# Zeros in more of TensorE's pauses, and filter spectra over even and odd tokens apart

## The reference, cut to what matters

```python
def hyena_filter_spectra(z, window, w1, b1, w2, b2, w3, b3, freq):
    h = sin(freq[0] * (z @ w1 + b1)); h = sin(freq[1] * (h @ w2 + b2))
    h = (h @ w3 + b3).reshape(L, HY_ORDER, 2, HY_WIDTH) * window[:, None, None, :]
    fwd, bwd = h[:, :, 0], h[:, :, 1]
    f = concatenate([fwd, zeros, bwd[1:][::-1]], axis=0)
    f = f / (sum(abs(f), axis=0, keepdims=True) + EPS)
    return rfft(f, axis=0)
```

## Time and profile before

| | |
|---|---|
| runs | 2994.73, 2994.0, 2991.17 us; median 2994.0 |
| profiled execution | 2988.92 us, span 2987.1 us |
| mean granted clock | 0.967 |
| busy share of the span | PE 94%, DVE 67%, ACT 51%, POOL 2% |

### The profile page before, as it was taken

One profiled execution on the slowest core, in us unless ns is written; L12 is line 12 of the kernel. 1 busy time (PEld: TensorE's weight loads), 2 busy tenths in 40 slices (PEclk: granted clock), 3 DMA queues, 4 the chain that ended last, 5 costly groups with the idle time before them and its releaser, 6 DMA issues. The chain is left out here.

```text
span 2987.1 us, 43738 instructions
## 1 busy us (share of the span) xinstructions
PE 2808.3 (94%) x17891; PEld 2482.1 (83%) x17891; DVE 2004.8 (67%) x2003; ACT 1514.4 (51%) x1456; POOL 68.8 (2%) x55
## 2 busy tenths in 40 slices
PE   5899998699999999999998989999899899989999
PEld 5799998588888888888886578999899788989898
DVE  6555565588888888888785466665555666666555
ACT  3444353466667676667663325444434326443442
POOL 1000000000000000000000210000000110000000
PEclk8899989699999999999999899999999999999999
DMA  6155540399999999999997234444355433444353
GB/s 188 61 180 192 177 155 16 121 365 331 368 329 349 347 334 364 328 366 334 340 356 233 94 97 127 142 155 142 113 178 190 147 111 102 150 147 141 127 186 110
DMA packets 365125, 619.40 MB, mean 207 GB/s; under 512 B 14664, under 2 KB 201127, under 8 KB 363701
## 3 DMA queue, kind: packets, MB, share of 16 engines
q1 hardware_dynamic: 363432, 611.77, 59.8%
q10 hardware_dynamic: 1550, 5.57, 0.5%
HBM read 611.93 MB, written 5.37 MB: 207 GB/s over the span
## 5 line engine op out<-in xcount | busy, mean ns | idle before, releaser
L366 DVE TENSOR_TENSOR slots_low<-slots,w_hi 128x2048 fp32r<-128x2048 f32 x240 | 549.5, 2293 | 379.4 <-ACT w_hi L355 379.2
L355 ACT ACTIVATE w_hi<-slots 128x2048 fp32r<-128x2048 f32 x240 | 452.8, 1891 | 335.9 <-PE ps L940 170.9
L1267 DVE TENSOR_TENSOR slots_low<-slots,w_hi 128x2048 fp32r<-128x2048 f32 x224 | 504.2, 2286 | 65.1 <-ACT w_hi L1218 65.1
L468 PE MATMUL ps<-x_hi,w_hi 128*128 128x256 f32 x1520 | 438.7, 289 | 51.5 <-DVE x_lo L548 26.7
L468 PE MATMUL ps<-x_lo,w_hi 128*128 128x256 f32 x1520 | 431.7, 284 | 0.0
L468 PE MATMUL ps<-x_hi,slots_low 128*128 128x256 f32 x1520 | 431.1, 284 | 0.0
L1218 ACT ACTIVATE w_hi<-slots 128x2048 fp32r<-128x2048 f32 x224 | 415.9, 1907 | 0.1
L1151 PE MATMUL ps<-slots_low,x_hi 128*128 128x512 f32 x896 | 352.1, 393 | 0.0
L468 PEld LDWEIGHTS ps<-x_hi,w_hi 128*128 128x128 f32 x1520 | 295.9, 195 | 59.4 <-issue 52.2
L468 PEld LDWEIGHTS ps<-x_lo,w_hi 128*128 128x128 f32 x1520 | 295.6, 194 | 0.3
L468 PEld LDWEIGHTS ps<-x_hi,slots_low 128*128 128x128 f32 x1520 | 295.3, 194 | 0.0
(11 more groups left out here) (536 smaller groups left out, 5374.0 us busy)
## 6 DMA issues: line engine op xcount, KB each, us to landing
slots<-in_moe_w_gate_dram SPq DMA_DIRECT2D x112, 1024.0 KB, 5.1
slots<-in_moe_w_up_dram SPq DMA_DIRECT2D x112, 1024.0 KB, 5.1
slots<-in_moe_w_down_dram SPq DMA_DIRECT2D x112, 1024.0 KB, 4.9
slots<-in_mlp_w_dram SPq DMA_DIRECT2D x64, 1024.0 KB, 5.2
slots<-in_w_in_dram SPq DMA_DIRECT2D x54, 1024.0 KB, 5.4
slots<-in_ffn_w_gate_dram SPq DMA_DIRECT2D x14, 1024.0 KB, 5.0
slots<-in_ffn_w_up_dram SPq DMA_DIRECT2D x14, 1024.0 KB, 5.0
slots<-in_ffn_w_down_dram SPq DMA_DIRECT2D x14, 1024.0 KB, 4.9
```

The costliest lines, as they stand in the source:

```text
L355: act.activation(w_hi[:, s.buffer, 0:s.kt * s.cols], slots[:, s.slot, 0:s.kt * s.cols], ACT.Copy).then_inc(w_hi_done, 1)
L366: dve.tensor_tensor(slots_low[:, s.slot, 0:n], slots[:, s.slot, 0:n], w_hi[:, s.buffer, 0:n].bitcast(F32), ALU.subtract).then_inc(w_lo_don ...
L468: mm = pe.matmul(b[:, t * T:(t + 1) * T], w, xx[:, k, :], **flags)
L1267: dve.tensor_tensor(low[i % NS], raw[i % NS], his[i % R].bitcast(F32), ALU.subtract).then_inc(lo_done, 1)
```

## The change

It adds `keep_busy` calls at some 25 places, gives `linear` an argument `idle` that does the same after its last matmul, lengthens the zeros at the end of `opening` from 50 to 80 matmuls, and rewrites `spectra`: PE transforms only the first half of the frequencies, even and odd tokens each into a bank of its own; ACT copies the even sums (into the buffer of `x_lo`, which gets a plain float32 name), and DVE forms both halves as sum and difference of odd and even (`join`). POOL clears the row that DVE cleared, and a unit's transforms stand behind 16 matmuls of zeros.

```diff
-        xl = sb(ctx, "x_lo", [P, KD, T], F32R)
+        x_lo_plain, xl = pinned(ctx, "x_lo", [P, KD, T])
...
+        def linear(srcs, items, extra=(), pool=None, hooks={}, side_banks=0, idle=0):
...  (after the last slab)
+                    if idle:
+                        if p >= NB:
+                            e = parts[p - NB][4]
+                            pe.wait_ge(act_emptied if e == "act" else dve_emptied, by[e].index(p - NB) + 1)
+                        keep_busy(pe, idle, p % NB)
...  idle= : first projection 26, q and kv 11, hyena projection 15, mix 13, cross q/k/v 13, each output projection but mLSTM's 5
...  keep_busy at the end of: rotate 16, spread 7, attention 4, mlp that doesn't store 12, first gather of experts 20,
...  opening 40 (was 25), mLSTM heads 14, ranks 46;  at the start of: mlp 3, opening 6, ranks 18
...  spectra, PE
+                        def transform(i, s, t):
+                            if i:
+                                if t == 0:
+                                    pe.wait_ge(evens_out, 2 * (i - 1) + s + 1)
+                                else:
+                                    pe.wait_ge(joined, 4 * (i - 1) + 2 * s + 2)
+                            if s == t == 0:
+                                if i:
+                                    pe.wait_ge(sized, i)
+                                keep_busy(pe, 8, 4)
                             pe.wait_ge(mixed, 2 * i + s + 1)
+                            pe.matmul(bank(4 + 2 * s + t), dft[:, t, s, 0:P], pq[i % 2][:, s, t, :], start=True, stop=True).then_inc(transformed, 1)
...
                         for i in range(N):
                             if i + 1 < N:
                                 make(i + 1)
+                            for s in range(2):
+                                for t in range(TT):
+                                    transform(i, s, t)
                             add_up(i)
+                        keep_busy(pe, 14, 0)
...  spectra, DVE: window(i+1), join(i, 0), mix(i+1), join(i, 1), size
+                        def join(i, s):
+                            if s == 0 and i:
+                                dve.wait_ge(spectra_out, 16 * i)
+                            dve.wait_ge(evens_out, 2 * i + s + 1)
+                            dve.wait_ge(transformed, 4 * i + 2 * s + 2)
+                            odd, even = bank(4 + 2 * s + 1), evens[:, s, :]
+                            dve.tensor_tensor(F[:, 2 * s, :], odd, even, ALU.add).then_inc(joined, 1)
+                            first, second = (even, odd) if s == 0 else (odd, even)
+                            dve.tensor_tensor(F[:, 2 * s + 1, :], first, second, ALU.subtract).then_inc(joined, 1)
...  spectra, POOL
+                            pool.wait_ge(windowed, 4 * i + 4)
+                            pool.memset(fb[0:1, 1, 0, :], 0.0).then_inc(lag0, 1)
...  spectra, ACT
+                            for s in range(2):
+                                act.wait_ge(transformed, 4 * i + 2 * s + 1)
+                                if i:
+                                    act.wait_ge(joined, 4 * (i - 1) + 2 * s + 2)
+                                act.activation(evens[:, s, :], bank(4 + 2 * s), ACT.Copy).then_inc(evens_out, 1)
                             if i + 1 < N:
                                 sizes(i + 1)
+                            act.wait_ge(joined, 4 * i + 4)
                             act.dma_start(spectra_dram[l][o], flat(F[:, :, :])).then_inc(spectra_out, 16)
```

More of the change, by code:

```diff
@@ L809, in _ @@
                             mix(i - 3)
+                    keep_busy(pe, 4)
                 @block.vector
@@ L969, in _ @@
                             mm.then_inc(turned, 1)
+                    if not store:
+                        keep_busy(pe, 12)
                 @block.scalar
@@ L1403, in spectra @@
                 F = sb(c, "spectra", [P, 4, 512])
+                evens = flat(x_lo_plain[:, 0:4, :]).rearrange("p (s n) -> p s n", s=2)
                 U = [(l, o) for l in range(2) for o in range(2)]
                 N = len(U)
[L1406 to L1407 removed]
+                with stage("made", "windowed", "lag0", "mixed", "absd", "added", "summed", "sized", "inverted", "transformed", "evens_out", "joined") as \
+                        (block, made, windowed, lag0, mixed, absd, added, summed, sized, inverted, transformed, evens_out, joined):
                     @block.tensor
@@ L1417, in make @@
                                               start=True, stop=True).then_inc(made, 1)
-                        def transform(i, n):
-                            s, k = n // 2, n % 2
-                            pe.wait_ge(mixed, 2 * i + s + 1)
[L1422 to L1426, removed]
+                        def transform(i, s, t):
[8 more added lines that the diff above has]
+                                keep_busy(pe, 8, 4)
+                            pe.wait_ge(mixed, 2 * i + s + 1)
+                            pe.matmul(bank(4 + 2 * s + t), dft[:, t, s, 0:P], pq[i % 2][:, s, t, :], start=True, stop=True).then_inc(transformed, 1)
                         def add_up(i):
                             pe.wait_ge(added, i + 1)
-                            if i:
-                                pe.wait_ge(outed, 4 * i)
+                            pe.wait_ge(evens_out, 2 * i + 1)
                             for m in range(4):
                                 for t in range(TT):
-                                    mm = pe.matmul(bank(7)[:, m:m + 1], ab[:, 0, t, m * P:(m + 1) * P], ones[:, 0:1], start=(t == 0), stop=(t == TT - 1))
+                                    mm = pe.matmul(bank(4)[:, m:m + 1], ab[:, 0, t, m * P:(m + 1) * P], ones[:, 0:1], start=(t == 0), stop=(t == TT - 1))
                             mm.then_inc(summed, 1)
@@ L1641, in layer @@
                             hooks["dve", j] = other_taps(*slabs)
-                        linear([x], pairs_of(0, [scale_to(hy[:, k:k + 2, 1:T + 1], rs) for k in range(0, 12, 2)]), ("first_tap", "second_tap", "convolved"), pool=pad, hooks=hooks)
+                        linear([x], pairs_of(0, [scale_to(hy[:, k:k + 2, 1:T + 1], rs) for k in range(0, 12, 2)]), ("first_tap", "second_tap", "convolved"), pool=pad, hooks=hooks, idle=15)
                         x.split = False
```

45 lines of the change are left out of this document (21 added, 24 removed).

## The result

The changed kernel takes 2971.5 us in the median of ten runs (2957.4 to 2982.8), the kernel before 2994.4 in ten (2991.2 to 3000.9): a ratio of 0.9913, 95% interval 0.9894 to 0.9933. It is faster by 23 us where 41 were forecast; the time lies inside the range (2939 to 2975), near its upper end. The profiled execution took 2973.2 us, span 2971.4, mean clock 0.982 (before 0.967).

What follows compares the result with a forecast made beforehand. TensorE, busy 94% of the span, was taken as the bound, its half-rate work counting twice. Terms summed to 38.4 us off the profiled 2988.9, giving 2950.5, carried to 2953 us; range 2939 to 2975.

Steps and rivals of the forecast that it cites:

- rotation, latent attention with its end zeros: Zeros around the rotation bring TensorE's 18.36 busy us at 0.50 to full clock: 9.2 us gained, 0.3 lost at attention's end.
- hyena, two: In two layers, 30 zeros (3.4 us) in a 4.4 us pause keep the clock: 3.1 us each, 6.2 gained.
- mix and the projection behind, two: Zeros at the mix's end, twice: 2.36 us gained, less 0.3 each by which 26 zeros outlast VectorE; 4.1 in all.
- row spreading (routing), experts: Routing: row spreading at full clock gains 3 us; 40 zeros behind the gather gain about 1 for the first expert's slab.
- the three folds: Three projections where TensorE waits for POOL's fold: the wait grows and the clock may fall, 2.7 us lost (bounds 0 and -5).
- attention's end, the other two: The 8 zeros at attention's end meet a pause of only 0.84 us: 0.3 us lost at each place.
- the second, latent attention staying slow: Rival: the long attention stretch stays at half rate despite the zeros, costing 9 us, 2962 us; chance 0.12.
- PEclk at 0.5 where zeros stand: Sign of being wrong: the added zeros themselves run at half rate.
- I let one of three fall: Spectra: of at most three clock falls at 5.1 us each, one is assumed, so 9 us gained instead of 14.
- the first rival: Spectra fall to half rate in every unit, taking the 9 us and one more: 2963 us; chance 0.14.
- zeros outlast their pauses: Rival: at stage ends the barrier waits for zeros, 1.4 us each at half of 25 sites: 3006 us; chance 0.06.
- the bound of -1: First projections: lower bound of the 1.2 us gain, where `spread`'s own 14 zeros run at half rate.

Runs made afterwards that it cites:

- zeros only: The changed kernel with the spectra of before and all the added zeros outside it: 2967.3 us, ratio 0.9901.
- zeros behind: The changed kernel with 12 of each spectra unit's 16 zeros taken from before the transforms, 12 put behind the first two units' sums: 2961.4 us, ratio 0.9881.
- sums between: The changed kernel without zeros in the spectra units, a unit's sums between its cosine and sine transforms: 2960.7 us, ratio 0.9872.
- spectra only: The kernel before with the new spectra alone, the 50 zeros in front left at 50: 3002.5 us, ratio 1.002.
- fold later: "zeros behind" plus the matmul over POOL's folded squares one tile later: 2959.0 us, ratio 0.9874.
- more zeros: "zeros behind" plus 24 more zeros behind the first projection and 8 in each of hyena's four pauses: 2952.2 us, ratio 0.9853.
- One zero: "combined" plus a single zero matmul before the second slab of second products in layer 0's MLP: 2942.1 us, ratio 0.9818.
- combined: "sums between" with sizes written behind the first join, the fold's matmul one tile later, and the added zeros of "more zeros": 2944.6 us, ratio 0.9844.

## Why the prediction came out as it did

Forecast of each term, and the gain by stages in us: in the pair of profiles, and as the difference of means over the four profiles that have the changed code there (changed, zeros only, zeros behind, sums between) and the two with the old (before, spectra only):

| term | forecast | pair | means |
|---|---|---|---|
| spectra | 9 | 6.1 | by the table above |
| rotation, latent attention with its end zeros | 9.2 - 0.3 | 8.1 | 7.5 |
| hyena, two | 6.2 | 1.8 | 5.0 |
| mix and the projection behind, two | 4.1 | 0.3 | 0.3 |
| cross attention, two | 3.4 | 2.9 | 2.9 |
| output projection and MLP, first block / layer 0 | 1.7 / 1.7 | 0.9 / -4.0 | 0.5 / -1.3 |
| the same in layer 1 | 0 | -1.6 | -0.2 |
| mLSTM heads and output | 1.45 | 1.0 | 1.7 |
| first projections, `spread`, q and kv | 1.2 | 0.6 | -1.3 |
| row spreading (routing), experts | 3 + 1 | 1.6 + 1.4 | 1.4 + 2.1 |
| the three folds | -2.7 | -4.2 | -2.5 |
| attention's end, the other two | -0.6 | -1.1 | -1.1 |

With some 2 us in the stages left out the pair's sum is 15.7 us. The medians differ by 23, as the profile before lies 5.5 us under its median and that after 1.7 above; the means come to some 16 without the spectra, 22 with the pair's 6.1.

The time lies in the range, but that is partly luck. The range's upper end was built from the first two rivals, and the second, latent attention staying slow, did not come. In the means the 16 us that are missing are spread: some 4 in the output projections and MLPs, 4 in the mix, 3 in the spectra, 2.5 in the first projections, the rest in small parts. Of the signs of being wrong "PEclk at 0.5 where zeros stand" came, in the spectra and in `spread`.

- **Spectra: the step that failed is "I let one of three fall".** The prices at full clock were right: joins 0.68 to 0.69 us, makes and transforms 3.60 us for eight, and with the clock up and 24 zeros fewer the stage takes 45.6 us, which by an estimate is 48.3 with these zeros (2.7 us) where 48 was worked out. But three falls came, 17.1 us at half rate: two in the make behind the sums, as in the first rival, and one behind the wait for the sizes, which the working has as a wait and not as a place for a fall. A fall's price was too high: 5.1 us in the working, some 2.6 by the 7.7 us above. So the stage gained 6.1 us with all three, where the working had 1 lost. Behind that is a comparison that I did not make: I set the new spectra at full clock against the old ones as they ran. The old ones behind the added zeros take 53.6, so those zeros are the gain and the rewrite, as it stands, a loss. In the better order it gains (45.6 to 47.8 us in four of five profiles).
- **Latent attention: right.** PEclk is 1.00 in both stages in every profile with the zeros. Halving was a little too much: 8.9 us with the end zeros taken off, 8.1 in the pair, 7.5 in the means.
- **Cross attention and mLSTM: right within half a us.**
- **Hyena: near in the mean (5.0 for 6.2), far off in the pair.** It takes 36.9, 38.6 or 40.3 us with no, one or two falls. The zeros at the projection's end leave the pause inside `hyena`, which I hadn't seen as one.
- **Mix: the rival "zeros outlast their pauses" in small.** They outlast VectorE by 0.58 us, not 0.3. The 2.0 us behind the barrier, while ACT and DVE split the next source, stay empty, and the clock fell there in six of eight cases.
- **First projections: the bound of -1 came true.** In the means it is -1.3, in the pair 0.6. The clock falls around the pause of 2.6 to 3.5 us that the 52 zeros leave, and `spread`'s own 14 zeros run in part or all at half rate: 4.0 to 4.7 us against 2.05. With 76 zeros it takes 2.7 in all five profiles, with 52 in one of seven ("fold later").
- **Fold: right in size (in the means) and cause.** The later matmul cures it clearly in layer 1, in layer 0 in four of five profiles; how much it gives in the mLSTM projection is open.
- **Layer 0's MLP: not in the working at all.** 4.6 us are lost in the pair, by the rhythm, 12% of the forecast sum. That the change brings on the slower rhythm is not shown: of the two profiles with the old code there, "before" has 187.7 us and "spectra only" 192.3.

The Trainium skill ("TensorE: Matmul & The Clock Gate", Part 1), weighed in the prediction, has a TensorE that stays busy return to its full rate. This case's trace disagrees: "spectra only" has TensorE 17.63 of 17.79 us busy, with sixteen 65-row makes and 16 zeros, at 0.50.

## What to carry over

Busy is not the same as keeping the clock. Look at which work stands where it falls: here it fell where one-column sums and 65-row makes followed each other, and not where 128-row transforms or zeros lay between them. Try another order before paying for fillers. Price a rewrite against the old code under the new surroundings, not as it ran. A filler paid here where it shortened the pause to 1.2 us (rotation) or closed it (inside hyena); where it left two us empty, as behind the mix, the clock fell in six of eight cases all the same and the filler cost its own tail. With steps of one or two us, several profiles of one stage tell more than the one pair, and more than a single profile of an experiment.

## What was not expected of the hardware

**Two rhythms at one clock.** Streams of fp32 matmuls of 128x256 ran at 113 or 118 ns each, both at PEclk 1.00. Layer 0's MLP shows it in its weight loads, 188 ns each or every third 192. The changed kernel:

```profile
L964 PEld LDWEIGHTS ps<-hidden_hi,w_hi 128*128 128x128 f32 x235 | 45.1, 192 | 0.0
L964 PEld LDWEIGHTS ps<-hidden_hi,slots_low 128*128 128x128 f32 x236 | 44.3, 188 | 0.0
L964 PEld LDWEIGHTS ps<-hidden_lo,w_hi 128*128 128x128 f32 x235 | 44.1, 188 | 0.0
```

"Zeros behind", with the same code there:

```profile
...
L964 PEld LDWEIGHTS ps<-hidden_hi,w_hi 128*128 128x128 f32 x236 | 44.3, 188 | 0.0
...
```

The stage took 192.3 or 186.5 us in these two. Without zero matmuls inside, seven of the ten profiles ran at 118; with them, both that were at 118 when it came changed at the first one. In the first block's MLP one zero matmul changed nothing. What sets the rhythm stays open.

**A fall that lasts.** The mLSTM heads took 23.6 to 24.9 us in the other profiles with their zeros, and 32.33 once ("more zeros"), at 0.68 with TensorE busy 30.26 us. "One zero" shows the like in the spectra, from the first make up to the third unit's make, and behind it:

```profile
1617.64:1640.60 22.96, 22.80 (x42) 11.29 (x43) 12.21 (x17) 5.08 (x6) 3.45 (x3) 0.55 0.00 0
1640.60:1672.57 31.97, 27.50 (x116) 15.58 (x114) 18.48 (x30) 7.37 (x11) 8.09 (x5) 0.95 0.41 165
```

The same order of work took 45.8 us in "combined": a fall that began in the first make cost 9 us.
